# A two-block transformer on one core: silu, mixed and residual tiles turned by VectorE and DMA instead of by TensorE

## What is computed

```
# block 1 (block 2 is alike, with three branches and other weights)
u      = rms_norm(h, norm_mix);  z = u @ w_in
mixed  = sum over n of sigmoid(gate_n) * (branch_n @ w_branch[n])   # 256 x 2048
h      = h + mixed @ w_out
v      = rms_norm(h, norm_ffn)
h      = h + (silu(v @ w_ffn_gate) * (v @ w_ffn_up)) @ w_ffn_down
out    = rms_norm(h, norm_final)        # between the blocks
```

## Time and profile before

| | us |
|---|---|
| median of 3 runs | 2964.18 |
| lowest and highest | 2962.78, 2964.36 |
| profiled execution, its own time | 2962.89 |
| its span in the trace | 2961.1 |
| mean granted TensorE clock | 1.0 (2.4 GHz) |

### The profile page before, as it was taken

How to read it: one execution, slowest core, us unless ns; L and a number is a source line. 1 busy time by engine, 2 the same in 40 slices (tenths; PEclk the granted TensorE clock), 3 DMA queues, 4 the chain that set the end, 5 groups by cost and what they waited for, 6 DMA issues and landing times.

```text
span 2961.1 us, 33191 instructions
## 1 busy us (share of the span) xinstructions
PE 2938.9 (99%) x13958; PEld 2454.1 (83%) x13958; DVE 1635.2 (55%) x1854; ACT 1368.3 (46%) x1833; POOL 63.3 (2%) x108
## 2 busy tenths in 40 slices
PE   8999999999999999999999999999999999999999
PEld 8998788888887888888888888888888888888887
DVE  5666665566555554555555544555555555445554
ACT  5545544444554443444456555444454444344443
POOL 1000000000011000000001000000000000000000
PEclk9999999999999999999999999999999999999999
DMA  7455455555576555555555445555555555555554
GB/s 267 161 182 183 171 189 178 206 198 189 185 244 217 189 194 188 197 185 189 193 179 199 159 172 180 182 178 190 187 186 194 187 187 193 189 198 185 186 197 156
DMA packets 84101, 561.77 MB, mean 190 GB/s; under 512 B 10067, under 2 KB 10211, under 8 KB 19056
## 3 DMA queue, kind: packets, MB, share of 16 engines
q1 hardware_dynamic: 77760, 544.80, 52.1%
q0 software_dynamic: 3456, 10.01, 1.2%
q10 hardware_dynamic: 2736, 4.83, 0.5%
HBM read 557.50 MB, written 3.68 MB: 190 GB/s over the span
## 4 chain that ended last, share of the span: by engine, by line
PE 97%; DVE 1%; DMA 1%; ACT 1%; issue 0%; POOL 0%; SPq 0%; DVEq 0%; ACTq 0%
PE acc L613 93%; PE misc L613 2%; PE misc L617 2%; DMA raw<-in_w_in 1%; DVE w_lo L1418 1%; ACT w_hi L990 0%; DMA lam_vec<-in_lam_vectors 0%; ACT prob L969 0%; ACT junk L977 0%; DVE lru_work L1661 0%; DVE turned L1418 0%; DVE prob L1424 0%; ACT L969 0%; ACT av L972 0%; DVE y_lru_lo L1418 0%
## 5 line engine op out<-in xcount | busy, mean ns | idle before, releaser
L1418 DVE TENSOR_TENSOR w_lo<-raw,w_hi 128x1024 fp32r<-128x1024 f32 x1032 | 1258.2, 1220 | 1076.2 <-ACT w_hi L990 1072.8
L990 ACT ACTIVATE w_hi<-raw 128x1024 fp32r<-128x1024 f32 x1032 | 1088.0, 1056 | 1216.9 <-PE acc L613 1214.9
L613 PE MATMUL acc<-w_hi,v_hi 128*128 128x512 f32 x1408 | 552.1, 392 | 0.0
L613 PE MATMUL acc<-w_hi,v_lo 128*128 128x512 f32 x1408 | 548.5, 390 | 0.0
L613 PE MATMUL acc<-w_lo,v_hi 128*128 128x512 f32 x1408 | 548.1, 389 | 0.0
L613 PE MATMUL acc<-w_hi,u_hi 128*128 128x512 f32 (+1 forms) x1248 | 494.2, 396 | 0.0
L613 PE MATMUL acc<-w_hi,u_lo 128*128 128x512 f32 (+1 forms) x1248 | 483.5, 387 | 0.0
L613 PE MATMUL acc<-w_lo,u_hi 128*128 128x512 f32 (+1 forms) x1248 | 482.7, 387 | 0.0
L613 PEld LDWEIGHTS acc<-w_hi,v_hi 128*128 128x128 f32 x1408 | 264.4, 188 | 56.2 <-issue 2.6
L613 PEld LDWEIGHTS acc<-w_hi,v_lo 128*128 128x128 f32 x1408 | 264.3, 188 | 55.6
L613 PEld LDWEIGHTS acc<-w_lo,v_hi 128*128 128x128 f32 x1408 | 264.5, 188 | 53.8
(11 more groups left out here) (313 smaller groups left out, 2808.8 us busy)
## 6 DMA issues: line engine op xcount, KB each, us to landing
raw<-in_w_gates SPq DMA_DIRECT2D x112, 1024.0 KB, 4.7
raw<-in_w_ffn_gate SPq DMA_DIRECT2D x88, 1024.0 KB, 4.7
raw<-in_w_ffn_up SPq DMA_DIRECT2D x88, 1024.0 KB, 4.7
raw<-in_w_ffn_down SPq DMA_DIRECT2D x88, 1024.0 KB, 4.6
raw<-in_w_in SPq DMA_DIRECT2D x67, 1024.0 KB, 4.7
raw<-in_w_out SPq DMA_DIRECT2D x32, 1024.0 KB, 4.7
raw<-in_w_branch SPq DMA_DIRECT2D x24, 1024.0 KB, 4.8
raw<-in_w_mem SPq DMA_DIRECT2D x8, 1024.0 KB, 4.7
```

Source lines behind the costliest of these rows:

```text
L613: return e.matmul(o, w, x, start=start, stop=stop, skip_group_check=True)
L990: e.activation(m.w_hi[:, n % PART_SLOTS, 0:HALF_KT * cols], m.raw[:, c % RAW_SLOTS, o * cols:(o + HALF_KT) * cols], ACT.Copy).then_inc(s[" ...
L1418: return e.tensor_tensor(o, a, b, op)
```

## The change

A move no longer touches TensorE or PSUM. In its place:

1. VectorE takes the 256 x 512 block (two tiles of 128 tokens) and transposes every 32x32 square in place of its own, two instructions of 128x512, and writes them sorted so that all squares bound for one partition quadrant are neighbours (`squares`).
2. ScalarE waits for them and issues 16 DMAs of 32 partitions x 256 fp32 (1 KB per partition), one for each pair of source and destination quadrant, from `squares` to `turned`, both in SBUF.
3. Two steps later ScalarE waits for all 16 to have landed and writes the high part; VectorE then writes the low part. Without a gain these are two instructions each of 128x512; with a gain ScalarE has four of 128x256 where it had eight of 128x128, VectorE eight of 128x128 as before.

The buffers `spare` lie over the two `silu` buffers, `mixed_turned` over parts of the branch outputs that are no longer needed. So the FFN's gate block j now waits for the move of j - 1, and its tanh waits for the low parts of that move (`moved_lo`). On TensorE a mover only lets its steps pass and notes for which count of `moved_lo` the tiles' readers wait. The last part of a move comes in its fourth step for hidden and residual tiles and in its fifth for mixed ones, where it was the second and the third.

```diff
 def parts_of(left):
-    return 1 if left in ("u", "mem", "y_lru", "y_diff", "y_win", "y_fox", "y_cross", "y_gqa") else 2
+    return 2 if left == "y_dil" else 1
+TURN_STEPS = 3
...
-                if j >= 2:
-                    lanes.finish(f"hidden_move:{mark}{half}{j - 2}")
+                if j:
+                    lanes.finish(f"hidden_move:{mark}{half}{j - 1}")
...
+        self.spare = [spot(f"spare{i}", q, 4 * i, [4, SEQ]) for i in range(2)]
+        self.mixed_turned = [spot(f"mixed_turned{i}", q, 24 + 4 * i, [4, SEQ]) for i in range(2)]
...
-    def put_tile(left, src, j, t, wait):
-        i, bank = tile_bank()
-        need(("ident_landed", 16))
-        need(wait)
-        transposes(bank, [tile(src, n) for n in range(4)], "tile_turned")
...
+    def moved(left, j):
+        yield TURN_STEPS
+        turn["moved"] += 1
         tiles = range(4 * j, 4 * j + 4)
         lanes.wrote(left, tiles)
         for k in tiles:
-            ready[left, k] = bank_free[i]
+            ready[left, k] = ("moved_lo", turn["moved"])
+        yield
...
+            e.wait_ge(s["moved_lo"], turn["moved"])
             sig = m.silu[i % 2]
             activate(sig[:, 0, :], v[:, 0, :], ACT.Tanh, scale=half_r[:, 0:1])
...
-    def put_tile(left, j, t, gain=None):
-        bank = m.bank[turn["turned"] % 2]
-        turn["turned"] += 1
-        hi, o = m.left[left][0], slice(t * P, (t + 1) * P)
-        e.wait_ge(s["tile_turned"], turn["turned"])
+    def moved(left, j, squares, turned, gain=None):
+        turn["moved"] += 1
+        hi = m.left[left][0]
+        yield
+        e.wait_ge(s["moved_turned"], turn["moved"])
+        for n in range(4):
+            for i in range(4):
+                e.dma_start(turned[32 * n:32 * n + 32, i, :], squares[32 * i:32 * i + 32, n, :]).then_inc(
+                    s["moved_landed"], 16)
+        yield TURN_STEPS - 1
+        e.wait_ge(s["moved_landed"], 256 * turn["moved"])
+        by_tile = turned[:, :, :].rearrange("p i (t m b) -> p t m i b", t=2, m=4)
         if gain is None:
-            i = activate(hi[:, 4 * j:4 * j + 4, o], bank[:, :].rearrange("p (a b) -> p a b", a=4), ACT.Copy)
+            for t in range(2):
+                o = hi[:, 4 * j:4 * j + 4, t * P:(t + 1) * P].rearrange("p m (i b) -> p m i b", i=4)
+                i = activate(o, by_tile[:, t, :, :, :], ACT.Copy)
         else:
             for k in range(4 * j, 4 * j + 4):
-                i = scaled(hi[:, k, o], tile(bank, k - 4 * j), m.gain(gain, k))
-        i.then_inc(s["tile_hi"], 1)
+                i = scaled(hi[:, k, :].rearrange("p (t i b) -> p t i b", t=2, i=4), by_tile[:, :, k - 4 * j, :, :],
+                           m.gain(gain, k))
+        i.then_inc(s["moved_hi"], 1)
...
+    def moved(left, j, tokens, squares, turned, gain=None):
+        for t in range(2):
+            to = squares[:, :, t * P:(t + 1) * P].rearrange("p n (m b) -> p m n b", m=4)
+            i = e.transpose(to, tokens[:, t, :].rearrange("p (m n b) -> p m n b", m=4, n=4))
+        i.then_inc(s["moved_turned"], 1)
+        yield TURN_STEPS
+        turn["moved"] += 1
         hi, lo = m.left[left]
-        e.wait_ge(s["tile_hi"], turn["tile"])
+        by_tile = turned[:, :, :].rearrange("p i (t m b) -> p t m i b", t=2, m=4)
+        e.wait_ge(s["moved_hi"], turn["moved"])
...
     def hidden_move(b, left, j, i):
-        for t in range(2):
-            put_tile(left, j, t)
-            yield
+        e.wait_ge(s[f"acc_freed{b.slot}"], b.after)
+        yield from moved(left, j, m.silu[j % 2][:, :, :], m.spare[(j + 1) % 2],
+                         m.spare[j % 2])
```

More of the change, by code:

```diff
@@ L585, in tensor_program @@
     bank_free = [None] * 4
-    turn = {"tile": 0, "task": 0, "hi": 0, "lo": 0}
+    turn = {"tile": 0, "task": 0, "hi": 0, "moved": 0}
     head_ready = {}
@@ L819, in mixed_move @@
         yield
-        done = ("mixed_added", (12 if mark else 0) + (4 if mark else 8) + c + 1)
-        for t in range(2):
-            put_tile("m" + mark, columns_of(m.mixed[:, t, :], c), c, t, done)
-            yield
+        yield from moved("m" + mark, c)
     def row_squares(b, j, left):
@@ L828, in resid_move @@
     def resid_move(b, j, left, gain):
-        for t in range(2):
-            put_tile(left, columns_of(m.resid[:, t, :], j), j, t, freed(b))
-            yield
+        yield from moved(left, j)
     def ffn_rows(mark):
@@ L836, in hidden_move @@
     def hidden_move(b, left, j, i):
-        for t in range(2):
-            put_tile(left, m.silu[j % 2][:, t, :], j, t, freed(b))
-            yield
+        yield from moved(left, j)
     def memory():
@@ L965, in scalar_program @@
     lanes = Lanes()
-    turn = {"turned": 0, "split": 0, "junk": None, "head_squares": 0}
+    turn = {"turned": 0, "moved": 0, "split": 0, "junk": None, "head_squares": 0}
     def activate(o, a, func, **kw):
@@ L1246, in mixed_move @@
         yield
-        for t in range(2):
-            put_tile("m" + mark, c, t)
-            yield
+        yield from moved("m" + mark, c, *m.mixed_turned)
     def row_squares(b, j, left):
@@ L1260, in resid_move @@
             e.wait_ge(s["gain12_done"], 1)
-        for t in range(2):
-            put_tile(left, j, t, gain)
-            yield
+        yield from moved(left, j, *m.spare, gain)
     def ffn_rows(mark):
@@ L1268, in hidden_move @@
     def hidden_move(b, left, j, i):
-        for t in range(2):
-            put_tile(left, j, t)
-            yield
+        yield from moved(left, j, m.spare[(j + 1) % 2], m.spare[j % 2])
     def memory():
@@ L1414, in vector_program @@
     lanes = Lanes()
-    turn = {"split": 0, "tile": 0, "lo": 0, "bank": 0, "total": 0}
+    turn = {"split": 0, "tile": 0, "moved": 0, "bank": 0, "total": 0}
     def tt(o, a, b, op):
@@ L1508, in evacuate @@
             stt(sig[:, 1, :], sig[:, 1, :], half_r2[:, 1:2], v[:, 1, :], ALU.mult, ALU.mult).then_inc(freed, 1)
-    def put_tile(left, j, t, gain=None):
-        bank = m.bank[turn["tile"] % 2]
-        turn["tile"] += 1
+    def moved(left, j, tokens, squares, turned, gain=None):
[5 more added lines that the diff above has]
+        turn["moved"] += 1
         hi, lo = m.left[left]
-        o = slice(t * P, (t + 1) * P)
-        e.wait_ge(s["tile_hi"], turn["tile"])
+        by_tile = turned[:, :, :].rearrange("p i (t m b) -> p t m i b", t=2, m=4)
+        e.wait_ge(s["moved_hi"], turn["moved"])
         if gain is None:
-            tiles = slice(4 * j, 4 * j + 4)
-            i = tt(lo[:, tiles, o], bank[:, :].rearrange("p (a b) -> p a b", a=4), hi[:, tiles, o].bitcast(F32),
-                   ALU.subtract)
+            for t in range(2):
+                o, x = (part[:, 4 * j:4 * j + 4, t * P:(t + 1) * P].rearrange("p m (i b) -> p m i b", i=4)
+                        for part in (lo, hi))
+                i = tt(o, by_tile[:, t, :, :, :], x.bitcast(F32), ALU.subtract)
         else:
             for k in range(4 * j, 4 * j + 4):
[L1522 to L1525, removed]
+                for t in range(2):
+                    o, x = (part[:, k, t * P:(t + 1) * P].rearrange("p (i b) -> p i b", i=4) for part in (lo, hi))
+                    i = stt(o, by_tile[:, t, k - 4 * j, :, :], m.gain(gain, k), x.bitcast(F32), ALU.mult, ALU.subtract)
+        i.then_inc(s["moved_lo"], 1)
         lanes.wrote(left, range(4 * j, 4 * j + 4))
+        yield
     def task_bank():
@@ L1844, in mixed_move @@
         yield
-        for t in range(2):
-            put_tile("m" + mark, c, t)
-            yield
+        e.wait_ge(s["mixed_added"], (12 if mark else 0) + (4 if mark else 8) + c + 1)
+        yield from moved("m" + mark, c, m.mixed[:, :, c * BW:(c + 1) * BW], *m.mixed_turned)
     def row_squares(b, j, left):
@@ L1854, in resid_move @@
             tt(m.gain12, m.gains[:, 2, :], m.gains[:, 3, :], ALU.mult).then_inc(s["gain12_done"], 1)
-        for t in range(2):
-            put_tile(left, j, t, gain)
-            yield
+        e.wait_ge(s[f"acc_freed{b.slot}"], b.after)
+        yield from moved(left, j, m.resid[:, :, j * BW:(j + 1) * BW], *m.spare, gain)
     def ffn_rows(mark):
```

6 lines of the change are left out of this document (2 added, 4 removed).

## The result

| | before | after |
|---|---|---|
| median | 2963.88 us | **3140.31 us** |
| lowest and highest, 4 runs each | 2962.78, 2964.36 | 3131.27, 3142.22 |
| span of the profiled execution | 2961.1 us | 3140.4 us |
| mean granted TensorE clock | 1.0 | 0.973 |

The changed kernel takes 1.059 times as long (95% interval 1.0569 to 1.0611). The forecast of 2933 us and its range were wrong, and in sign: 176 us were lost where 31 were expected to be won.

A forecast was written before the change was run, and what follows sets the result against it. TensorE's own queue was taken as the bound: 2962.9 - 39.3 for removed transposes + 7.6 for tile waits + 1 for residual moves = 2932, and 2933 us with the median 1.3 above; range 2924 to 2968.

The forecast's parts named there:

- The 39.3 us on TensorE: Removing 336 transposes, 42 moves at 0.93 or 0.94 us each, takes 39.3 us off TensorE's queue.
- VectorE's transposes: Two square transposes of 128x512 per move on VectorE, 0.686 us each, with 1.22 as upper bound.
- E + 4.0: In a hidden move, ScalarE gets its squares 4.0 us after E, the end of the block just computed on TensorE.
- The window of 7.15 us for 16 issues: ScalarE can issue a hidden move's 16 DMAs in 7.15 us, 0.447 each, before its next w_hi is late.
- The price of an issue: Each DMA issue on ScalarE's queue takes 0.40 us, so 16 take 6.4 us with 0.75 us of window left.
- upper bound of 0.47: Highest issue price in the 0.36 to 0.47 us range for ScalarE, the pitch of issues at the program's start.
- Rival (c): Slow issues on ScalarE push back and spend the gain: 2990 us at 0.52 each, near 3260 at 0.93; chance 0.18.
- break-even of 0.49 us: Issue price on ScalarE above which the 0.93 us gained per move is spent: 7.8 us against the 7.15 window.
- case of 0.52: ScalarE issues at 0.52 us overrun the window by 1.17 us in each of 42 moves, giving 2990 us.
- Four tile waits, 7.6 us: TensorE waits for the last mixed tiles 2.3 us twice and the last output-projection tiles 1.5 us twice, together 7.6.
- Landings (3.2 us) and weights: Moved data lands 3.2 us after issue, hidden in hidden moves; late weight loads keep 1.7 us of cover, costing nothing.
- rival (b): Late landing of the moved data beside weight traffic: near 2949 us, chance 0.13, or near 2966 us, chance 0.04.

The follow-up runs named there:

- split88: The changed kernel with eight of each move's sixteen issues on ScalarE's queue and eight on SP's: 2929.70 us, ratio 0.9887 to the kernel before.
- cal: The kernel before with groups of DMAs added behind its last store, differing in source, rows, queue and waiting, to price an issue; its whole time means nothing.
- split133: The changed kernel with thirteen of each move's sixteen issues on ScalarE's queue and three on SP's: 3014.28 us, ratio 1.0171 to the kernel before.
- hbm5: The changed kernel with squares stored to HBM by one DMA and loaded by four, low parts one half later: 2972.69 us, ratio 1.0031 to the kernel before.

## Why the prediction was wrong

**The 39.3 us on TensorE: right.** split88's span comes out within 1 us of the sum that has 0.93 us for each of the 42 moves, and no new work stood in their place.

**VectorE's transposes: right.** 0.686 us taken, 0.690 and 0.687 measured. ScalarE got its squares at E + 3.9, forecast at E + 4.0: the block ends at 1316.6 in the chain, the first issue is at 1320.49. The row of the hidden tiles:

```profile
L1517 DVE STREAM_TRANSPOSE spare<-silu 128x512 f32<-128x512 f32 x44 | 28.6, 690 | 0.0
```

**The window of 7.15 us for 16 issues: right**, shown twice: 16 x 0.64 − 7.15 = 3.1 us each and 3.15 measured in the mean, 13 x 0.64 − 7.15 = 1.2 and 1.0 to 1.24 measured in most.

**The price of an issue: the step that failed.** I took 0.40 us from the earlier trace rows, all of which have HBM at one end; the changed kernel's row is

```profile
L1083 ACTq DMA_DIRECT2D spare<-spare x544: 513/612/1629, 761.9 to 3036.3; - x182
...
DMA to landing us min/median/max: 1.8/1.9/6.3
```

and the pitch 0.64. ScalarE's rows are right in themselves: cal gives 0.34 for such a load alone and 0.44 in a row. The upper bound of 0.47 was drawn from the same kind of DMA, so the whole range missed what differed: SBUF at both ends. I also took a value below the only rows in which issues did follow one another at once on this queue, on the ground that mine had fewer rows each. cal shows that fewer rows save nothing here. My estimate from a figure of the Trainium skill (DMA: Bandwidth & Descriptors), 0.43 us, is about that of HBM issues in a row and 0.2 short of this case.

**Rival (c) named the right mechanism, with the wrong reason and the wrong price.** I tied it to outstanding data pushing back, and argued against it from small pieces. cal has no weight traffic and the same 0.61, and 0.51 with nothing outstanding at all. At 0.64 its own sum would have been 2933 + 42 x 3.1 + 4 (m_lo at 11.7, no v_lo) = 3067 us. Its break-even of 0.49 us an issue was not run. split133 is near its case of 0.52: thirteen issues at 0.64 take 8.3 us, as sixteen at 0.52 do, and the time was 3014 where (c)'s sum has 2990, since that held neither the slow clock (18 us) nor the 0.163 us that each wait hides (6.9). Why SP's issues in the earlier trace rows took 0.91 and 1.57 us with HBM at one end, no run settles; so pressure from outstanding weights is ruled out for this move's issues, and not for those.

**The clock: the term that no case held, and the second step that failed.** The other 72 us are matmuls at 1.2 GHz behind the waits. I had costed a wait at its own length throughout. Before, the trace has a single long wait, at the start; none of its waits in mid-stream exceeds 1.8 us, so the trace of before had no row from which to take this price, and I did not bound it.

**Four tile waits, 7.6 us: mis-sized.** 11.7 in the changed kernel, where the m_lo waits grew with the late issues and those for v_lo vanished; I take it that TensorE, held back by w_lo in the same moves, no longer arrived early. In split88, where issues are on time, they are 5.3.

**Landings (3.2 us) and weights: on the safe side.** 1.9 in the median for hidden and residual tiles, 2.4 for mixed ones; 3.1 in split88, where the median is close to my 3.2. They were hidden but for one place in split88: a DMA issued at 809.2 landed 7.1 us later, ScalarE waited 4.5 us for it, and the 3.3 us for v_lo follow there. That is rival (b)'s mechanism, once in 42 moves. ScalarE waited for raw weights only once in the changed kernel, 0.8 us for in_w_in.

## What to carry to other kernels

Count a DMA's issue as an instruction of the engine that issues it, price it by a row with the same source *and* destination memory, and multiply by the longest run of issues that stands ahead of work somebody waits for. Where the run is longer than the lead, spread it over two queues before anything else: here that turned 3140 us into 2930, and better than spreading it in time, which delays the data. And where a change makes TensorE wait in the middle of a stream, look at the granted clock behind the waits: here waits near 1 us cost their length, and 42 waits of 2.7 to 6 us cost half as much again in slow matmuls behind them.

## What the runs showed of the hardware

- SBUF-to-SBUF DMAs cost ScalarE's queue 0.51 us alone and 0.61 in a row (pitch 0.64), SP's 0.59 in a row; loads from HBM on ScalarE's queue 0.34 and 0.44 (cal), a store to HBM 0.345 (hbm5); on GpSimd's queue eight SBUF-to-SBUF ones took 3.99 us, 0.50 each. Rows (32 or 128: 0.612 or 0.622) and bytes (1 or 2 KB a row: 612 or 613 ns) make next to no difference, and ScalarE's and SP's queues issue at once nearly as fast as by themselves (5.07 and 5.30 us for eight each, SP's alone 4.94). The Trainium skill (DMA: Bandwidth & Descriptors, Issuing engines are not separate DMA queues) says that more queues only save time on the sequencer, "which is usually small relative to the DMA itself"; that they save the sequencer's time agrees with the rows. That it is small did not hold here: sixteen issues took 10.2 us on one queue and half of it on two, against landings of 1.9, and that decided the kernel.
- In the changed kernel, behind 37 of 42 waits of 2.67 to 5.96 us TensorE's matmuls started 0.43 us apart (granted clock 0.50, 1.2 GHz) for 6 to 14 instructions; behind five of 2.67 to 3.06 us none did. In split133 none did behind waits of up to 1.62 us, and 7 or 8 did behind seven of eight waits of 1.9 to 2.7 us. In split88 a wait of 3.3 us for v_lo had none behind it. No run here separates the length of one wait from what else TensorE did around it.
- Adding 504 unneeded matmuls in front of those waits made the kernel 57 us faster.
